# The first slab of the input projection is multiplied with tiles that are not yet normalised

## The chip, the cores and the metric

The kernel runs on one core of a Trainium2 chip. The metric is the device time of one execution in microseconds (us); the shown number is the median of three runs. The engines of the core work side by side, each on its own list of instructions, and wait for each other on semaphores: TensorE (PE, matmuls into the eight PSUM banks), VectorE (DVE), ScalarE (ACT), GpSimd (POOL) and SyncE (SP, which issues the loads of weights).

## The reference

Two transformer-like blocks follow each other on one sequence of 512 tokens and 1024 features in fp32. The part around the change is the end of the first block and the beginning of the second:

```python
# first block, end
x = x + 0.5 * swiglu(rmsnorm(x, ffn2_norm), ffn2_w_gate, ffn2_w_up, ffn2_w_down)
x = rmsnorm(x, final_norm)
# second block, beginning
mod = silu(c) @ ada_w + ada_b                 # shift, scale and gate for each feature
h = rms_norm(x, mix_pre_g) * (1.0 + sc_m) + sh_m
p = h @ w_in                                  # 1024 x 2848: 23 slabs of 128 columns
# rmsnorm(x, g) = x * rsqrt(mean(x*x) + 1e-6) * g, the mean over the features of a token
```

The columns of p feed a gated convolution with 31 taps and, after a mix of each token with the one before it, a recurrence (three lora inputs, then r, k and v).

## The kernel before, in words

**Layout.** Everything lies feature by token: `xT` is eight tiles (KD) of 128 features x 512 tokens. A weight slab is 128 x 1024: the eight 128x128 blocks that make one output tile of 128 columns. Each product is made to nearly fp32 precision from rounded parts: a weight slab is split into `w_hi` and `w_lo`, an activation tile into `h_hi` and `h_lo`, and each block takes three matmuls (hi x hi, hi x lo, lo x hi; `passes`, lines 730 to 732). A slab so costs 24 matmuls of 512 columns.

**Weights.** SP loads slabs into a ring of four; slab n is requested when slab n - 4 has counted up `slab_done`. GpSimd splits each one in order (lines 600 and 602, `w_split`). The slabs of the stretch are `down2` (24: three for each of the eight output tiles), then `in2` (23).

**The seam.** `down(...)` runs the last projection of the first block. Output tile m goes to bank m % 4; VectorE adds it to `xT` (`add_half`, line 2081), ScalarE squares it (`norm_squares`, line 1551), VectorE adds the squares up. When tile 7 is squared, TensorE finishes the sums (`last_sums`, line 850). Two norms follow each other here with nothing between, so their two scales for a token are found together: ScalarE takes the roots (1608, 1609), VectorE the reciprocals (1972, 1974), and TensorE spreads the product of both over the partitions into bank 6 (line 861, `spread`). VectorE scales the tiles with it (`norm_split`, line 2006), ScalarE adds the shift and rounds to `h_hi` (`norm_hi`, line 1627), VectorE makes `h_lo` (line 1996). Tile by tile, `first(2, ...)` multiplies the first two slabs of `in2` (lines 762, 763, 768) into banks 0 and 1; at its end it spreads the scale of the first norm alone into bank 5 ("the second spread").

**Behind it.** `for m in range(2, 23): project(m)` multiplies the other slabs with 24 matmuls each (bank m % 4, lines 730 to 732), and `lora_products(2 * (m - 3), 2 * (m - 3) + 2)` follows `project(m)` for m from 3 to 8 (line 1259). The very first of them waits so:

```python
if n == 0:
    pe.wait_ge(S("lora_in"), 48)
    pe.wait_ge(S("lora_act"), 3)
...
if n == 0:
    pe.wait_ge(S("x_final"), 8)
```

`x_final` counts eight `final_norm` tiles that VectorE makes from `xT` and bank 5 (line 2475). VectorE then clears four margins (2481) and runs `shifted(0)` to `shifted(2)` (line 2266), which finish the three lora inputs that ScalarE has copied out of banks 0, 1 and 2 (`raw_in`, line 1751). ScalarE applies a tanh and two sigmoids to them (lines 1876 to 1878, with two table loads) and counts `lora_act` to 3. All orders are written out by hand; every engine works its list strictly in order.

Of the kernel before, what the change touches and what calls it, by code (L numbers as in the profile page):

```python
# [18 lines left out]
P = 128  # L19
# [61 lines left out]

HI_AT = {"ffn1": 0, "mix": 1, "ffn2": 2, "mixpre": 3, "ffnpre": 4}

# [147 lines left out]
def build(nc, x_in, slabs, ada_in, vec_in, both_in, block1_in, block2_in, rope_in, relb_in, lora_in, g2b_in,  # L231
          y_out):
    ctx = ExitStack()
    with ctx:
# [31 lines left out]
        masks_t = place("masks", 3 * P, F32R, offset=g2b_at)  # L266
        ones_t = masks_t[:, :].bitcast(F32)
        arena = cursor[0]
        acth_t, actl_t = place("act_hi", KF * T, F32R), place("act_lo", KF * T, F32R)
# [4 lines left out]
        masks = {n: masks_t[:, P * i:P * i + P] for i, n in enumerate((64, 32, 128))}  # L274
        act_hi, act_lo = tiles(acth_t, KF), tiles(actl_t, KF)

        def slot(name, at, n, dt=F32, w=T):
# [84 lines left out]
        row_rec = small_t[:, 108:124]  # L362
        keep_mu = small_t[:, 60:75]
        d_end, omka = [small_t[:, 28 + 16 * half:44 + 16 * half] for half in range(2)], small_t[:, 232:236]

# [361 lines left out]
        def _(pe):  # L727
# [20 lines left out]

            def first(count, at, norm, wait_bank, late=None):


                for k in range(KD):
                    if late == "mix" and k == 5:
                        norm_stats(late)
                    for n in range(count):
                        if k == 0:
                            wait_bank(n)
                            pe.wait_ge(S("w_split"), at + n + 1)
                        if n == 0:
                            pe.wait_ge(S("norm_hi"), 8 * HI_AT[norm] + k + 1)  # L760
                        w, r = slice(P * k, P * k + P), (at + n) % RING
                        mm(bank[n], w_hi[:, r, w], h_hi[:, k, :], start=k == 0, stop=False, skip_group_check=True)  # L762
                        mm(bank[n], w_lo[:, r, w], h_hi[:, k, :], start=False, stop=False, skip_group_check=True)  # L763

                    pe.wait_ge(S("norm_lo"), 8 * HI_AT[norm] + k + 1)
                    for n in range(count):
                        w, r = slice(P * k, P * k + P), (at + n) % RING
                        last = mm(bank[n], w_hi[:, r, w], h_lo[:, k, :], start=False, stop=k == KD - 1, skip_group_check=True)  # L768
                        if k == KD - 1:
                            last.then_inc(S("slab_done"), 1)  # L770
# [153 lines left out]
            def down(name, o, done, done_at, norm):  # L924
# [23 lines left out]
                if norm == "ffnpost":  # L948
                    last_row_by_halves()
                    return  # L950
                last_sums(norm)
                pe.wait_ge(S("second_rs"), 1)
                spread(bank[6], both_rs, 1).then_inc(S("second_mm"), 1)


# [502 lines left out]


            first(2, at, "mixpre", lambda n: pe.wait_ge(S("x_new"), 21 + n))  # L1460
            for m in range(2, 23):
                project(m)
# [80 lines left out]
        def _(act):  # L1543
            f = nc.scalar.activation

            def norm_squares(name, src, wait=None):
# [32 lines left out]
                else:  # L1579
                    for j in range(KD - 1 if name == "ffnpost" else KD):  # L1580
# [8 lines left out]
                        if name not in LATE and j == KD - 2:  # L1589

                            f(small_t[:, 254:255], small_t[:, 255:256], ACT.Sqrt)
                        square(j)
                if name == "ffnpost":
                    for half in range(2):
# [12 lines left out]
                if name == "mixpre":  # L1607
                    f(both_std, pre_sums[1], ACT.Sqrt, bias=EPS * EPS, scale=1.0 / D).then_inc(S("second_std"), 1)
                f(n_std, pre_sums[0] if name == "mixpre" else bank[7][:, 0:4], ACT.Sqrt, bias=EPS, scale=1.0 / D)\
                    .then_inc(S("norm_std"), 1)  # L1610

            def late_hi(name, j):
# [127 lines left out]
            for i in range(2):  # L1740
                act.dma_start(lora[:, i, :], lora_in[:, i, :]).then_inc(S("lora_in"), 16)
            norm_hi("mixpre")


            def raw_in(m):
# [3 lines left out]
                if m == 0:  # L1749
                    act.wait_ge(S("keep_mu"), 1)  # L1750
                f(shift_tile(m), bank[n % 4], ACT.Copy, scale=keep_mu[:, mu_of(m):mu_of(m) + 1]).then_inc(S("in2_raw"), 1)
# [192 lines left out]
        def _(dve):  # L1944
# [116 lines left out]
            def gains_made():  # L2061
# [11 lines left out]
                v.tensor_tensor(gp["mixpost"], mod[:, 16:24], vec("mix_post_g", 0, 8), ALU.mult)  # L2073
                v.tensor_tensor(gp["ffnpost"], mod[:, 40:48], vec("ffn_post_g", 0, 8), ALU.mult)

            def add_half(o, at, n_slabs, scale, norm):

                for m in range(KD):
                    sum_squares(norm, m - 1)
                    dve.wait_ge(S("slab_done"), at + n_slabs * (m + 1))  # L2080
                    v.scalar_tensor_tensor(out=xT[:, m, :], in0=bank[m % 4][:, :], scalar=scale, in1=xT[:, m, :],  # L2081
# [172 lines left out]
            gains_made()  # L2254
            add_half(16, SLAB_AT["down2"], 3, 0.5, "mixpre")

            dve.wait_ge(S("block1_in"), 32)
            norm_split("mixpre", gs["mixpre"])
            v.tensor_scalar(keep_mu, vec("mu", 0, 15), -1.0, 1.0, ALU.mult, ALU.add).then_inc(S("keep_mu"), 1)
            link(v.tensor_scalar(omka, vec("k_a", 0, 4), -1.0, 1.0, ALU.mult, ALU.add))  # L2260

# [92 lines left out]
            def recurrence(half):  # L2354
# [97 lines left out]
                if half:  # L2452
                    dve.wait_ge(S("second_std"), 2)
                    for j in range(4):
# [275 lines left out]
```

## Time and profile before

| | |
|---|---|
| median of 3 runs | 1700.24 us (1700.13 to 1701.5) |
| the profiled execution | 1701.04 us, of which the span from first to last instruction is 1699.2 us |
| TensorE busy | 1657.6 us, 98% |
| VectorE, ScalarE, GpSimd busy | 56%, 25%, 58% |
| mean granted clock of TensorE | 0.991 |

Busy times are shares of the span. A matmul's end is modelled and matmuls overlap, so the distance between the starts of two matmuls is the measure of their cost and not the duration shown. The granted clock of a stretch is 1.00 at 2.4 GHz and 0.50 at 1.2 GHz.

### The profile page before, as it was taken

Reading aid. Unit: us, or ns where it says so; the run is one execution under the profiler, and the core shown is the slowest. Engines: PE = TensorE matmul, PEld = TensorE weight load, DVE = VectorE, ACT = ScalarE, POOL = GpSimd, SP = SyncE. Lnnn points to the kernel's source line nnn. Section 1 sums busy time; section 2 is a strip of 40 time slices with the busy share of each in tenths; the row PEclk is TensorE's granted clock in tenths of the full one; section 3 lists DMA queues with packets and bytes.
Section 4 is the critical chain, followed back from the end, with each engine's and each line's share of the span. In section 5 each row is a group of like instructions: output and inputs, shape, how many; then the busy total and the mean of one; then the engine's idle time right before and its main releaser. Section 6 shows DMA issues by size and latency. Waiting matters only on the chain.

```text
span 1699.2 us, 26804 instructions
## 1 busy us (share of the span) xinstructions
PE 1657.6 (98%) x10118; PEld 1355.5 (80%) x10118; DVE 946.7 (56%) x1389; ACT 433.2 (25%) x721; POOL 981.4 (58%) x596
## 2 busy tenths in 40 slices
PE   8999999999999999999999999998989999999998
PEld 6888888888767778888888867887868788888887
DVE  5666551226656346666562159987766766665103
ACT  4000000015866321111100031234353333233001
POOL 3666666766572377666677744611205576666774
PEclk9999999999999999999999989999999899999999
DMA  6444443333241134444443322210002232233332
GB/s 215 142 147 148 146 144 118 102 100 121 87 120 33 50 106 143 142 147 148 148 150 111 100 87 70 92 64 3 3 2 87 75 96 92 97 99 99 101 110 88
DMA packets 52112, 175.43 MB, mean 103 GB/s; under 512 B 6272, under 2 KB 8704, under 8 KB 51904
## 3 DMA queue, kind: packets, MB, share of 16 engines
q1 hardware_dynamic: 43056, 144.64, 26.3%
q10 hardware_dynamic: 8976, 29.63, 5.5%
q8 instruction: 61, 1.00, 0.3%
q14 instruction: 19, 0.16, 0.0%
HBM read 169.46 MB, written 2.10 MB: 101 GB/s over the span
## 4 chain that ended last, share of the span: by engine, by line
PE 93%; ACT 2%; DVE 2%; issue 1%; POOL 1%; DMA 0%; ACTq 0%; SPq 0%; DVEq 0%; POOLq 0%
PE banks L730 25%; PE banks L732 25%; PE banks L731 25%; PE banks L1199 4%; PE banks L1055 1%; PE banks L1028 1%; PE banks L762 1%; PE banks L1039 1%; PE banks L763 1%; PE banks L768 1%; PE banks L850 1%; PE banks L1025 1%; PE banks L1174 1%; PE banks L803 1%; PE banks L805 0%
## 5 line engine op out<-in xcount | busy, mean ns | idle before, releaser
L602 POOL TENSOR_TENSOR w_lo<-w_raw,w_hi 128x1024 fp32r<-128x1024 f32 x256 | 634.2, 2477 | 21.4
L600 POOL TENSOR_SCALAR w_hi<-w_raw 128x1024 fp32r<-128x1024 f32 x256 | 288.4, 1126 | 555.5 <-DMA w_raw<-in_slabs 477.0
L730 PE MATMUL banks<-h_hi,w_hi 128*128 128x512 f32 x1376 | 540.6, 393 | 0.6 <-POOL w_lo L602 0.6
L732 PE MATMUL banks<-h_hi,w_lo 128*128 128x512 f32 x1376 | 535.7, 389 | 0.0
L731 PE MATMUL banks<-h_lo,w_hi 128*128 128x512 f32 x1376 | 535.6, 389 | 0.0
L730 PEld LDWEIGHTS banks<-h_hi,w_hi 128*128 128x128 f32 x1376 | 258.4, 188 | 60.2 <-issue 5.8
L731 PEld LDWEIGHTS banks<-h_lo,w_hi 128*128 128x128 f32 x1376 | 258.4, 188 | 54.4 <-issue 1.7
L732 PEld LDWEIGHTS banks<-h_hi,w_lo 128*128 128x128 f32 x1376 | 258.3, 188 | 54.1
L730 PE MATMUL banks<-act_hi,w_hi 128*128 128x512 f32 (+1 forms) x550 | 209.7, 381 | 0.0
L731 PE MATMUL banks<-act_lo,w_hi 128*128 128x512 f32 (+1 forms) x550 | 209.3, 381 | 0.0
L732 PE MATMUL banks<-act_hi,w_lo 128*128 128x512 f32 (+1 forms) x550 | 209.3, 381 | 0.0
L730 PEld LDWEIGHTS banks<-act_hi,w_hi 128*128 128x128 f32 x550 | 103.4, 188 | 19.7
L731 PEld LDWEIGHTS banks<-act_lo,w_hi 128*128 128x128 f32 x550 | 103.4, 188 | 19.7
L732 PEld LDWEIGHTS banks<-act_hi,w_lo 128*128 128x128 f32 x550 | 103.4, 188 | 19.7
L2041 DVE TENSOR_TENSOR tmp<-banks,tmp 128x512 f32<-128x512 f32 x44 | 30.5, 692 | 148.2 <-PE banks L732 144.6
L1633 ACT ACTIVATE tmp<-tmp 128x512 f32<-128x512 f32 x44 | 27.9, 634 | 329.5 <-DVE tmp L2041 329.4
L2081 DVE SCALAR_TENSOR_TENSOR xT<-banks,xT 128x512 f32<-128x512 f32 x24 | 16.5, 690 | 165.4 <-PE banks L732 165.4
L2033 DVE TENSOR_TENSOR act_lo<-tmp,act_hi 128x512 f32 x66 | 103.9, 1574 | 8.1
L2055 DVE CUSTOM_DVE_ANT_0 adaw<-adaw,silc 128x1024 f32<-128x1024 f32 x48 | 78.9, 1643 | 5.1 <-DMA adaw<-in_ada 4.8
L2599 DVE SCALAR_TENSOR_TENSOR tmp<-banks,vec,tmp 128x511 f32<-128x511 f32 x44 | 32.8, 746 | 75.9 <-ACT tmp L1933 75.8
L1199 PEld LDWEIGHTS banks<-in_arena 64*64 64x64 f32 x1792 | 59.5, 134 | 10.5 <-issue 6.9
L1199 PE MATMUL banks<-in_arena 64*64 64x64 f32 (+1 forms) x1792 | 62.3, 231 | 5.6 <-issue 2.7
(389 smaller groups left out, 1840.8 us busy)
## 6 DMA issues: line engine op xcount, KB each, us to landing
w_raw<-in_slabs SPq DMA_DIRECT2D x260, 512.0 KB, 3.5
adaw<-in_ada ACTq DMA_DIRECT2D x48, 512.0 KB, 3.6
relb<-in_relb ACTq DMA_DIRECT2D x8, 256.0 KB, 2.9
out_y<-xT SPq DMA_DIRECT2D x16, 128.0 KB, 1.8
w_raw<-in_slabs SPq DMA_DIRECT2D x4, 256.0 KB, 5.2
xT<-in_x SPq DMA_DIRECT2D x1, 1024.0 KB, 8.3
block<-in_block ACTq DMA_DIRECT2D x1, 704.0 KB, 6.1
xT<-in_x SPq DMA_DIRECT2D x2, 256.0 KB, 3.8
```

Of the source, the lines that this page charges most:

```text
L600: nc.gpsimd.tensor_scalar(w_hi[:, r, :], w_raw[:, r, :], 1.0, 1.0, ALU.mult, ALU.mult).then_inc(S("w_hi"), 1)
L602: nc.gpsimd.tensor_tensor(w_lo[:, r, :], w_raw[:, r, :], w_hi[:, r, :], ALU.subtract).then_inc(S("w_split"), 1)
L730: mm(out, hi, rhs_hi, start=start, stop=False, skip_group_check=True)
L731: mm(out, hi, rhs_lo, start=False, stop=False, skip_group_check=True)
L732: return mm(out, lo, rhs_hi, start=False, stop=stop, skip_group_check=True)
L762: mm(bank[n], w_hi[:, r, w], h_hi[:, k, :], start=k == 0, stop=False, skip_group_check=True)
L1199: last = mm(out, block_of(lhs, operands, e, g, c), r, start=opens and i == 0, stop=i == len(pairs) - 1, skip_group_check=True)
L1633: f(tmp[:, 2 + u, :], tmp[:, 2 + u, :], ACT.Silu).then_inc(S("silu"), 1)
L2033: v.tensor_tensor(actl_t[:, bass.ds(at * T, T)], t, hi, ALU.subtract).then_inc(S("act_lo"), 1)
L2041: v.tensor_tensor(tmp[:, 2 + u, :], bank[2 * u], tmp[:, 0, :], ALU.mult).then_inc(S("gate_scaled"), 1)
L2055: v.tensor_tensor_reduce(out=adaw[:, u, :], in0=adaw[:, u, :], in1=silc, scale=1.0, scalar=0.0, op0=ALU.mult, op1=ALU.add, accum_out=mod_s ...
L2599: v.scalar_tensor_tensor(out=tmp[:, n, 1:T], in0=bank[n][:, 0:T - 1], scalar=w[1], in1=tmp[:, n, 1:T], op0=ALU.mult, op1=ALU.add).then_inc ...
```

## The change

Slab 0 of `in2` is no longer multiplied with the normalised tiles. ScalarE and VectorE make tiles `act_hi` and `act_lo` from `xT` times the feature's gain alone (`unscaled_hi`, `unscaled_lo`), seven of them before the last down projection's tile is added, the eighth after it. TensorE multiplies slab 0 with them in four places between the steps of the norm (`first_unscaled`), then multiplies the slab with the shift, two columns (`shift_parts`, 16 matmuls), into bank 3. ScalarE copies bank 3's columns and bank 0 out, VectorE multiplies bank 0 with the scale in bank 6 and adds the shift's product. `first` then takes slabs 1 and 2 into banks 1 and 2, and the loop of projections begins at slab 3. `raw_in(0)` and product 3 wait for the repaired bank.

```diff
-HI_AT = {"ffn1": 0, "mix": 1, "ffn2": 2, "mixpre": 3, "ffnpre": 4}
+HI_AT = {"ffn1": 0, "mix": 1, "ffn2": 2, "unscaled": 3, "mixpre": 4, "ffnpre": 5}
...
                 if norm == "ffnpost":
                     last_row_by_halves()
                     return
+                first_unscaled(range(2))
                 last_sums(norm)
+                first_unscaled(range(2, 3))
                 pe.wait_ge(S("second_rs"), 1)
                 spread(bank[6], both_rs, 1).then_inc(S("second_mm"), 1)
+                first_unscaled(range(3, KD))
+                n = SLAB_AT["in2"]
+                for k in range(KD):
+                    w = slice(P * k, P * k + P)
+                    for part in (w_hi, w_lo):
+                        last = mm(bank[3][:, 0:2], part[:, n % RING, w], shift_parts[:, k, :], start=k == 0 and part is w_hi,
+                                  stop=k == KD - 1 and part is w_lo, skip_group_check=True)
+                last.then_inc(S("slab_done"), 1)
+
+            def first_unscaled(ks):
+                n = SLAB_AT["in2"]
+                if 0 in ks:
+                    pe.wait_ge(S("x_new"), 21)
+                    pe.wait_ge(S("w_split"), n + 1)
+                for k in ks:
+                    w = slice(P * k, P * k + P)
+                    pe.wait_ge(S("norm_hi"), 8 * HI_AT["unscaled"] + k + 1)
+                    pe.wait_ge(S("norm_lo"), 8 * HI_AT["unscaled"] + k + 1)
+                    passes(bank[0], w_hi[:, n % RING, w], w_lo[:, n % RING, w], act_hi[:, k, :], act_lo[:, k, :], k == 0, k == KD - 1)
...
-            first(2, at, "mixpre", lambda n: pe.wait_ge(S("x_new"), 21 + n))
-            for m in range(2, 23):
+            first(2, at + 1, "mixpre", lambda n: pe.wait_ge(S("x_new"), 22 + n), begin=1)
+            for m in range(3, 23):
+                if m == 3:
+                    pe.wait_ge(S("keep_mu"), 2)
                 project(m)
...
                         square(j)
+                        if name == "mixpre" and j == KD - 2:
+                            act.wait_ge(S("slab_done"), SLAB_AT["down2"] + 3 * (KD - 1) + 1)
+                            for i in range(KD - 1):
+                                unscaled_hi(i)
+                        if name == "mixpre" and j == KD - 1:
+                            unscaled_hi(j)
...
+            def unscaled_hi(j):
+                f(act_hi[:, j, :], xT[:, j, :], ACT.Copy, scale=gs["mixpre"][:, j:j + 1]).then_inc(S("norm_hi"), 1)
...
             norm_hi("mixpre")
+            act.wait_ge(S("slab_done"), SLAB_AT["in2"] + 1)
+            f(shift_sums, bank[3][:, 0:2], ACT.Copy)
+            f(tmp[:, 0, :], bank[0], ACT.Copy).then_inc(S("second_std"), 1)
...
                 if m == 0:
-                    act.wait_ge(S("keep_mu"), 1)
+                    act.wait_ge(S("keep_mu"), 2)
...
+                link(v.tensor_copy(shift_parts[:, :, 0], shf["mixpre"]))
+                link(v.tensor_tensor(shift_parts[:, :, 1], shf["mixpre"], shift_parts[:, :, 0], ALU.subtract))
+
+            def unscaled_lo(j):
+                dve.wait_ge(S("norm_hi"), 8 * HI_AT["unscaled"] + j + 1)
+                v.scalar_tensor_tensor(out=act_lo[:, j, :], in0=xT[:, j, :], scalar=gs["mixpre"][:, j:j + 1], in1=act_hi[:, j, :],
+                                       op0=ALU.mult, op1=ALU.subtract).then_inc(S("norm_lo"), 1)
...
                     sum_squares(norm, m - 1)
+                    if norm == "mixpre" and m == KD - 1:
+                        for j in range(KD - 1):
+                            unscaled_lo(j)
                     dve.wait_ge(S("slab_done"), at + n_slabs * (m + 1))
...
             add_half(16, SLAB_AT["down2"], 3, 0.5, "mixpre")
+            unscaled_lo(KD - 1)
             dve.wait_ge(S("block1_in"), 32)
             norm_split("mixpre", gs["mixpre"])
             v.tensor_scalar(keep_mu, vec("mu", 0, 15), -1.0, 1.0, ALU.mult, ALU.add).then_inc(S("keep_mu"), 1)
+            dve.wait_ge(S("second_std"), 2)
+            v.tensor_tensor(shift_sum, shift_sums[:, 0:1], shift_sums[:, 1:2], ALU.add)
+            link(v.tensor_tensor(bank[0], tmp[:, 0, :], bank[6], ALU.mult))
+            v.tensor_scalar(bank[0], bank[0], shift_sum, None, ALU.add).then_inc(S("keep_mu"), 1)
```

In `first` the new argument `begin` moves the banks (`bank[begin + n]`); the rest of the diff places the small tiles and moves a later wait on `second_std` from 2 to 3.

## Rows read from the trace of the kernel before

**Rows 1.** The page: engine totals, and the chain that ended last by engine.

```profile
PE 1657.6 (98%) x10118; PEld 1355.5 (80%) x10118; DVE 946.7 (56%) x1389; ACT 433.2 (25%) x721; POOL 981.4 (58%) x596
...
PE 93%; ACT 2%; DVE 2%; issue 1%; POOL 1%; DMA 0%; ACTq 0%; SPq 0%; DVEq 0%; POOLq 0%
```

**Rows 2.** Timeline of TensorE: start, duration, what, count, idle before and its releaser.

```profile
975.60 1.84 PE L850 MATMUL banks<-small,tmp 128*128 128x2 f32 x16
...
977.30 0.49 PE L730 MATMUL banks<-act_hi,w_hi 128*128 128x512 f32 x1
...
979.70 1.87 PE L850 MATMUL banks<-small,tmp 128*128 128x3 f32 x8 [1.45 <-ACT tmp L1551]
...
982.11 1.12 PE L861 MATMUL banks<-both,small 128*128 128x128 f32 x4 [0.54 <-DVE small L1972]
...
984.92 0.77 PE L762 MATMUL banks<-h_hi,w_hi 128*128 128x512 f32 x1 [1.69 <-ACT h_hi L1627]
...
990.88 0.39 PE L762 MATMUL banks<-h_hi,w_hi 128*128 128x512 f32 x1
...
997.69 0.60 PE L861 MATMUL banks<-both,small 128*128 128x128 f32 x4
...
998.04 0.48 PE L730 MATMUL banks<-h_hi,w_hi 128*128 128x512 f32 x1
...
1008.81 0.39 PE L732 MATMUL banks<-h_hi,w_lo 128*128 128x512 f32 x1
...
1009.59 1.13 PE L1259 MATMUL banks<-in_arena 64*128 64x512 f32 x4 [0.39 <-issue]
```

**Rows 3.** Timelines of VectorE, ScalarE and GpSimd through the seam.

```profile
978.29 0.69 DVE L2081 SCALAR_TENSOR_TENSOR xT<-banks,xT 128x512 f32<-128x512 f32 x1 [12.57 <-PE banks L732]
...
979.02 0.63 ACT L1551 ACTIVATE tmp<-xT 128x512 f32<-128x512 f32 x1 [15.44 <-DVE xT L2081]
...
981.88 0.18 DVE L1972 RECIPROCAL small<-small 128x4 f32<-128x4 f32 x1 [2.90 <-ACT small L1608]
...
983.27 1.41 DVE L2006 SCALAR_TENSOR_TENSOR tmp<-xT,mod,banks 128x512 f32<-128x512 f32 x2 [1.15 <-PE banks L861]
...
984.05 1.38 ACT L1627 ACTIVATE h_hi<-tmp,mod 128x512 fp32r<-128x512 f32 x2 [2.21 <-DVE tmp L2006]
...
984.81 0.98 DVE L1996 SCALAR_TENSOR_TENSOR h_lo<-tmp,mod,h_hi 128x512 fp32r<-128x512 f32 x1
...
993.71 1.63 DVE L1996 SCALAR_TENSOR_TENSOR h_lo<-tmp,mod,h_hi 128x512 fp32r<-128x512 f32 x2
...
977.06 2.36 POOL L602 TENSOR_TENSOR w_lo<-w_raw,w_hi 128x1024 fp32r<-128x1024 f32 x1
```

**Rows 4.** Timelines of VectorE and ScalarE behind the second spread.

```profile
998.39 5.36 DVE L2475 SCALAR_TENSOR_TENSOR xT<-xT,vec,banks 128x512 f32<-128x512 f32 x8 [2.62 <-PE banks L861]
...
1005.62 0.74 DVE L2266 SCALAR_TENSOR_TENSOR tmp<-banks,vec,tmp 128x511 f32<-128x511 f32 x1
...
1007.05 1.28 ACT L1877 ACT_TABLE_LOAD   x1
...
1008.88 0.61 ACT L1878 ACTIVATE tmp<-tmp 128x512 f32<-128x512 f32 x1
```

**Rows 5.** Windows of TensorE: stretch, length, busy (count), granted clock, DMA, GB/s.

```profile
978.00:978.50 0.50, 0.26 (x2) 0.98 0.00 0
...
978.50:979.00 0.50, 0.00 (x0) 0.50 0.00 0
...
988.50:989.00 0.50, 0.50 (x3) 0.78 0.00 0
```

**Rows 6.** Windows: busy of PE, PEld, DVE, ACT, POOL, then granted clock.

```profile
1016.00:1126.00 110.00, 110.00 (x459) 84.42 (x459) 101.62 (x144) 25.96 (x41) 53.44 (x31) 1.00 0.27 87
```

**Rows 7.** The chain, a piece of it: start, duration, first matmul at the next norm.

```profile
1324.94 0.77 PE banks L762
```

**Rows 8.** Windows of all engines, at the next norm.

```profile
1330.00:1331.00 1.00, 1.00 (x5) 0.83 (x5) 1.00 (x3) 0.50 (x1) 0.47 (x1) 0.97 0.00 0
```

## What the change will do to the time: the prediction

> **What bounds the kernel now.** I read the engine table and the chain of waits first. TensorE is busy 98% of the span and is 93% of the chain [rows 1], so only TensorE time can be won, and the question is what each stretch of it waits for. Then I went through TensorE's timeline at the seam between the last down projection and the input projection [rows 2], next to VectorE's and ScalarE's [rows 3], to see who ends each wait. The last big product starts at 977.30 and three such matmuls with their start-up end near 978.1. The next big matmul starts only at 984.92. In those 6.8 us stand: the add of tile 7 (978.29), its square (979.02), the sums (979.70, 1.87 us), root and reciprocal (981.88), the spread (982.11), the first scaled tile (983.27) and its rounding (984.05). The granted clock [rows 5] is at its low level, 0.50 (1.2 GHz), from 978.5 and comes back only at about 988.7: the windows row 988.50 to 989.00 has 0.78. From 984.92 to 988.7 TensorE works at half speed, so 3.8 us cost 1.9. The visible price of the seam is 6.8 + 1.9 = 8.7 us. That is what the change aims at.
>
> Then I asked what stands behind the seam, because an earlier product is worth something only if what follows can start. The row that decides is L1259, the first lora product, at 1009.59 with 0.39 us of idle before it [rows 2]. The profile calls that "issue". The code has a wait there for lora_act (three activations) and x_final. On the other engines [rows 4] the third activation starts at 1008.88 and lasts 0.61, so it ends at 1009.49, 0.10 us before the product. Its chain goes back without a hole: the spread into bank 5 starts at 997.69 [rows 2]; VectorE starts the eight final-norm tiles at 998.39 and has them at 1003.75; four memsets and three shifted tiles follow, the last from 1005.62 to 1006.36; then tanh, a table load at 1007.05 (1.28), two sigmoids. So L1259 starts 1009.59 - 997.69 = **11.9 us after the spread starts**, whatever TensorE does in between. Now it has two products in between (2 and 3), 0.35 + 2 x 5.44 = 11.2 us, plus a little, and waits 0.4 to 0.55.
>
> **The change part by part.** One matmul of 512 columns costs 0.227 us at the full clock: from 990.88 to 997.69 lie five steps of six, 1.362 each [rows 2].
>
> *Before the sums.* ScalarE makes seven unscaled hi tiles (0.7 each, 5.0 us) and VectorE seven lo tiles (0.75 to 1.0 each, at most 7 us) after the first slab of row 7 is used. That slab is done 39 matmuls before 975.60, at 966.8, so lo is through at about 974.7. VectorE stood idle 12.57 us before 978.29 and ScalarE 15.44 us before 979.02 [rows 3], so this costs nothing; without that cover the add of tile 7 would be late by what is over. The two small operations that make shift_parts fall before the down projection, where VectorE waits for TensorE. The weight slabs that the seam needs are split by 977.06 + 2.36 = 979.42 at the latest [rows 3] and the first of them well before.
>
> *TensorE through the seam, at full clock.* Two unscaled steps, 6 x 0.227 = 1.36: 978.1 to 979.45. The sums wait for the same square as before: 979.70, now at the fast price of row 975.60 (1.70 for 16, so 0.85 for 8): 980.55. The third step with 0.1 start-up, 0.78: 981.33. ScalarE inserts hi 7 after the square (0.7), and VectorE inserts lo 7 (0.98 as in row 984.81) from 980.4 to 981.4. That stands ahead of its reciprocals, which would be due near 980.8, so it delays them by 0.6 and the spread starts at 981.65 (0.23 behind the reciprocal as now). Spread 0.35: 982.0. Five steps, 3.4 + 0.1: 985.5. The shift's product is 16 matmuls of two columns. The trace has this form only as the sums, 0.106 each, so 1.7; below, it may vanish almost (0); above, it is bounded by a full matmul each, 3.6. I take 1.7, the nearest in columns: 987.2. Then the two-slab loop over scaled tiles, 8 x 1.362 = 10.9, which ends at 998.1. The scaled tiles no longer bound it: the first scaling starts at 982.35 instead of 983.27, the last lo tile is there near 994.4 instead of 995.34 [rows 3] and is wanted at 997.6. So the second spread starts at **998.1, against 997.69: 0.4 us later**, with three slabs done at that point instead of two. This is a gain of 5.44 - 0.4 = 5.0 us of TensorE work.
>
> *Repair of bank 0.* ScalarE adds two copies, VectorE three operations (about 0.16 + 0.7 + 0.75), from 994.8 to 996.5; product 3 waits for it but starts at 998.45. Cover 1.9 us; a longer repair would delay product 3, which has room, as follows. Slab in2+4 is requested earlier, when the shift's product ends, which only helps.
>
> *After the spread.* Only product 3 is left between the spread and L1259: 998.45 to 1003.9. The lora chain starts with the spread at 998.1 and is not shortened by anything in the diff, so L1259 starts at 998.1 + 11.9 = 1010.0, and TensorE stands idle **6.1 us** where it stood 0.4. Queued behind L1259 are product 4 and all others; none can pass. The 5.0 us are thus returned in full, and 0.4 us more. From 1016 to 1126 TensorE is busy 110.00 of 110 us and VectorE 101.62 [rows 6], so lateness there is not taken in later.
>
> *The clock.* The stall is followed by slow matmuls. The trace has two such restarts: 984.92 to 988.7 (3.8 us, costs 1.9), and at the next norm from 1324.94 to about 1330.0, where the windows row 1330 to 1331 has 0.97 [rows 5, 7, 8] (5.1 us, costs 2.5). I take 2.25 for the new stall. The stall's length, 6.1, is near the 6.7 between 978.3 and 984.9 in which the clock stayed low.
>
> The Trainium skill ("TensorE: Matmul & The Clock Gate", HAM oscillation) says that a wait between two bursts throttles the engine again, so that the next burst starts slow; rows 5 agree (0.50 through the wait, and 3.8 us into the next burst). By that rule the change moves the slow restart instead of removing it. The same page (What's actually happening) says the number of slow matmuls varies from run to run; two restarts of 3.8 and 5.1 us in one trace fit that.
>
> **Sum.** 0.4 + 2.25 = 2.65 us. Against the profiled execution, 1701.04 (span 1699.2 and 1.84 around it), this is 1703.7; that execution is 0.8 above the median of the runs, 1700.24, from which it is 1702.9. I take the middle, **1703.3**. What a measurement can tell from no change is 0.2%, 3.4 us, so from 1700.24 the line lies at 1703.64, just above.
>
> **The rivals.**
> *A. The clock falls within the seam as well.* For: in rows 5 it fell by 978.5, only 0.2 us after the last big matmul ended, so the idle time behind cannot have done it alone; the 16 small matmuls from 975.60 stand unchanged, and the change adds 16 more at 985.5. Against: 978.1 to 979.45 is now filled. Slow steps cost 1.9 to 2.5 once more, all before the second spread and therefore all on the path: 1705.2 to 1706.3 (1703.3 + 1.9 to 2.5, and a little for a product of 3.0 instead of 1.7). Chance 0.32.
> *B. As intended.* The place is L1259: if its wait is not the lora chain but something that moves along with TensorE, product 4 follows product 3 at once, 5.0 us are gained and no restart is slow: 1700.24 - 5.0 = 1695.2; with some part of the stall left, up to 1699. Against: 0.10 us between the end of the sigmoid and the product, and a chain without holes [rows 4]. This decides from the point where lora_act is ready before 1003.9. Chance 0.06.
> *C. The stall costs only its 0.4.* The slow restart is short or the shift's product nearly free: 1700.2 to 1702.2. For: low bound 0 of that product. Against: both restarts of the trace. Chance 0.14.
> *D. The new work on VectorE and ScalarE is dearer than its cover* (lo tiles past 978.29, or a table load for the copies between squares and roots): 1 to 3 us on the path, 1704.3 to 1706.5. Against: 12.57 us of idle time, and copies behind the roots that had no load. Chance 0.05.
>
> **How the numbers follow.** The forecast (0.43) has its own range, 1702.3 to 1704.3; a quarter of it lies above 1703.64. Faster by over 0.2% (under 1696.8): most of B, and a rest for what I have missed: 0.06. Slower: A 0.30, D 0.05, the quarter of the forecast 0.11, in all 0.46. Within 0.2%: 0.48. The range, 1701.2 to 1706.5, takes in A, D and the upper half of C, and leaves B out.
>
> **What would show it.** L1259 after more than 5 us of idle time; the last activation 0.1 us before it; the second spread within 1 us of 997.7; the granted clock high through 979 to 998 (low there: A) and low after 1004; no idle time of note before the first unscaled matmul. I am wrong if product 4 follows product 3 closely, if lora_act comes before 1004, or if the 16 two-column matmuls take more than 3 us.

## The result, and the profile after

The kernel after takes 1708.26 us (median of 5 runs, 1707.33 to 1709.45), the kernel before 1700.24 us beside it: the ratio is 1.0045, 95% interval 1.0034 to 1.0056, slower by 8.0 us. Forecast were 1703.3 us and a range of 1701.2 to 1706.5. The direction and the stall came as forecast; the size did not: 1708.26 us lies outside the range.

The page of the kernel after, engine totals [for before: rows 1]:

```profile
PE 1663.5 (98%) x10134; PEld 1355.4 (79%) x10134; DVE 963.8 (57%) x1402; ACT 439.5 (26%) x731; POOL 989.0 (58%) x596
```

TensorE's timeline of the kernel after through the seam and behind it (start, duration, what, count, idle before and its releaser). The lines answer to rows 2; L855 is line 850 of before, L866 is 861, L1286 is 1259, L733 to L735 are 730 to 732, and L966 is the shift's product:

```profile
977.63 1.84 PE L855 MATMUL banks<-small,tmp 128*128 128x2 f32 x16
...
982.64 0.48 PE L733 MATMUL banks<-act_hi,w_hi 128*128 128x512 f32 x1
...
983.43 0.60 PE L866 MATMUL banks<-both,small 128*128 128x128 f32 x4
...
987.32 0.17 PE L966 MATMUL banks<-shift_parts,w_hi 128*128 128x2 f32 x1
...
989.02 0.48 PE L766 MATMUL banks<-h_hi,w_hi 128*128 128x512 f32 x1
...
996.63 0.39 PE L767 MATMUL banks<-h_hi,w_lo 128*128 128x512 f32 x1
997.34 0.74 PE L772 MATMUL banks<-h_lo,w_hi 128*128 128x512 f32 x2 [0.33 <-DVE h_lo L2038]
...
1000.73 0.60 PE L866 MATMUL banks<-both,small 128*128 128x128 f32 x4
1001.49 0.50 PE L733 MATMUL banks<-h_hi,w_hi 128*128 128x512 f32 x1 [0.16 <-DVE banks L2317]
...
1006.84 0.39 PE L735 MATMUL banks<-h_hi,w_lo 128*128 128x512 f32 x1
1012.74 2.08 PE L1286 MATMUL banks<-in_arena 64*128 64x512 f32 x4 [5.51 <-ACT tmp L1920]
1014.75 0.79 PE L733 MATMUL banks<-h_hi,w_hi 128*128 128x512 f32 x1
```

Three things are to be seen. The seam is closed: between 977.63 and 1000.73 TensorE has no hole of more than half a microsecond (the longest is the 0.33 us at 997.34). Three slabs are done at the second spread (1000.73). Then L1286 waits 5.51 us, and the profile now names ScalarE's last activation as the releaser. ScalarE, VectorE and GpSimd in the same execution, in three timelines [rows 3 and 4]. L2038 makes the lo tiles of the norm, L2048 scales a tile with bank 6:

```profile
1003.42 1.28 ACT L1918 ACT_TABLE_LOAD   x1
1009.55 0.63 ACT L1918 ACTIVATE in_arena<-in_arena 64x512 f32<-64x512 f32 x1 [4.85 <-DVE tmp L2324]
1010.20 1.28 ACT L1919 ACT_TABLE_LOAD   x1
...
1012.03 0.62 ACT L1920 ACTIVATE tmp<-tmp 128x512 f32<-128x512 f32 x1
```

```profile
969.66 8.76 DVE L2123 SCALAR_TENSOR_TENSOR act_lo<-xT,mod,act_hi 128x512 fp32r<-128x512 f32 x7 [2.12 <-ACT act_hi L1649]
980.32 0.69 DVE L2134 SCALAR_TENSOR_TENSOR xT<-banks,xT 128x512 f32<-128x512 f32 x1 [1.89 <-PE banks L735]
...
985.61 2.37 DVE L2038 SCALAR_TENSOR_TENSOR h_lo<-tmp,mod,h_hi 128x512 fp32r<-128x512 f32 x1
...
993.02 1.46 DVE L2038 SCALAR_TENSOR_TENSOR h_lo<-tmp,mod,h_hi 128x512 fp32r<-128x512 f32 x1
994.51 0.75 DVE L2048 SCALAR_TENSOR_TENSOR tmp<-xT,mod,banks 128x512 f32<-128x512 f32 x1
995.17 2.11 DVE L2038 SCALAR_TENSOR_TENSOR h_lo<-tmp,mod,h_hi 128x512 fp32r<-128x512 f32 x1
...
1001.54 5.36 DVE L2533 SCALAR_TENSOR_TENSOR xT<-xT,vec,banks 128x512 f32<-128x512 f32 x8
...
1008.77 0.74 DVE L2324 SCALAR_TENSOR_TENSOR tmp<-banks,vec,tmp 128x511 f32<-128x511 f32 x1
```

```profile
985.02 2.42 POOL L605 TENSOR_TENSOR w_lo<-w_raw,w_hi 128x1024 fp32r<-128x1024 f32 x1
...
994.02 2.71 POOL L605 TENSOR_TENSOR w_lo<-w_raw,w_hi 128x1024 fp32r<-128x1024 f32 x1
```

The last activation ends at 1012.65 and L1286 starts at 1012.74, 12.0 us after the second spread: it was 11.9 before. The windows of TensorE (stretch, length, busy, granted clock, DMA, GB/s) show where the clock is low [rows 5]:

```profile
982.00:1000.00 18.00, 17.68 (x90) 1.00 0.22 79
1004.00:1011.00 7.00, 3.23 (x15) 1.00 0.34 119
1011.00:1012.00 1.00, 0.00 (x0) 0.58 0.00 0
1012.00:1013.00 1.00, 0.26 (x2) 0.50 0.00 0
1017.00:1018.00 1.00, 1.00 (x4) 0.51 0.00 0
```

It is at 1.00 through the whole seam, and still until 1011, though the last matmul before the stall started at 1006.84. It falls to 0.50 within the stall and is back only near 1018.0, so L1286 takes 2.0 us instead of 1.06 and the first matmuls of product 4 0.43 instead of 0.23.

**Where the 6.3 us between the two spans lie** (1705.5 - 1699.2). Take the start of an instruction in the trace of after minus the start of the same one before:

| instruction | before | after | difference |
|---|---|---|---|
| a product of the first slabs | 12.29 | 11.51 | -0.78 |
| down projection 1, early | 293.89 | 293.42 | -0.47 |
| a product on cq_lo, in the attention behind it | 410.68 | 411.12 | +0.44 |
| the 16 sums of rows 2 | 975.60 | 977.63 | +2.03 |
| the first lora product | 1009.59 | 1012.74 | +3.15 |
| product 4 | 1010.65 | 1014.75 | +4.10 |
| the same product, clock back | 1012.16 | 1017.48 | +5.32 |
| the last down projection, late | 1646.30 | 1652.75 | +6.45 |

The seam and its stall account for 3.3 us (2.03 to 5.32). About 2.8 us are lost before it, from 12 to 976 us, and 1.1 behind it. There the diff changes no instruction on the path. The difference grows evenly inside the three down projections, by 0.9 to 1.2 us in each, by some 0.5 us in the attention between the first two, and hardly anywhere else. That asked for the experiments.

### The profile page after: what moved, and what is told of

It reads as the page before. It is cut to its first block, busy times and chain, and to the rows that moved or that the text cites. A ratio compares the mean times of both kernels' runs of the same rounds, so it can differ in the third digit from the quotient of the medians.

```text
span 1705.5 us, 26870 instructions
## 1 busy us (share of the span) xinstructions
PE 1663.5 (98%) x10134; PEld 1355.4 (79%) x10134; DVE 963.8 (57%) x1402; ACT 439.5 (26%) x731; POOL 989.0 (58%) x596
## 4 chain that ended last, share of the span: by engine, by line
PE 90%; DVE 4%; ACT 3%; POOL 2%; issue 1%; DMA 1%; ACTq 0%; SPq 0%; DVEq 0%; POOLq 0%
PE banks L733 25%; PE banks L735 25%; PE banks L734 25%; PE banks L1226 4%; PE banks L1055 1%; PE banks L1082 1%; PE banks L855 1%; PE banks L766 1%; PE banks L772 1%; PE banks L1066 1%; PE banks L767 1%; DMA w_raw<-in_slabs 1%; PE banks L1201 1%; DVE h_lo L2038 1%; PE banks L808 0%
## 5 line engine op out<-in xcount | busy, mean ns | idle before, releaser
L603 POOL TENSOR_SCALAR w_hi<-w_raw 128x1024 fp32r<-128x1024 f32 x256 | 293.5, 1147 | 554.0 <-DMA w_raw<-in_slabs 475.9
L733 PE MATMUL banks<-h_hi,w_hi 128*128 128x512 f32 x1368 | 538.2, 393 | 0.7 <-POOL w_lo L605 0.5
L735 PE MATMUL banks<-h_hi,w_lo 128*128 128x512 f32 x1368 | 533.0, 390 | 0.0
L733 PEld LDWEIGHTS banks<-h_hi,w_hi 128*128 128x128 f32 x1368 | 257.2, 188 | 61.5 <-issue 6.5
L735 PEld LDWEIGHTS banks<-h_hi,w_lo 128*128 128x128 f32 x1368 | 257.1, 188 | 54.0
L733 PE MATMUL banks<-act_hi,w_hi 128*128 128x512 f32 (+1 forms) x558 | 215.3, 386 | 0.0
L735 PE MATMUL banks<-act_hi,w_lo 128*128 128x512 f32 (+1 forms) x558 | 213.8, 383 | 0.0
L735 PEld LDWEIGHTS banks<-act_hi,w_lo 128*128 128x128 f32 x558 | 104.7, 188 | 22.6
L733 PEld LDWEIGHTS banks<-act_hi,w_hi 128*128 128x128 f32 x558 | 104.9, 188 | 19.2
L2134 DVE SCALAR_TENSOR_TENSOR xT<-banks,xT 128x512 f32<-128x512 f32 x24 | 16.6, 691 | 161.0 <-PE banks L735 161.0
L2075 DVE TENSOR_TENSOR act_lo<-tmp,act_hi 128x512 f32 x66 | 100.0, 1514 | 8.1
L2088 DVE TENSOR_TENSOR tmp<-tmp 128x512 f32<-128x512 f32 x44 | 65.3, 1484 | 8.6 <-ACT tmp L1672 8.6
```

The source lines that it names most:

```text
L603: nc.gpsimd.tensor_scalar(w_hi[:, r, :], w_raw[:, r, :], 1.0, 1.0, ALU.mult, ALU.mult).then_inc(S("w_hi"), 1)
L733: mm(out, hi, rhs_hi, start=start, stop=False, skip_group_check=True)
L735: return mm(out, lo, rhs_hi, start=False, stop=stop, skip_group_check=True)
L2075: v.tensor_tensor(actl_t[:, bass.ds(at * T, T)], t, hi, ALU.subtract).then_inc(S("act_lo"), 1)
L2088: v.tensor_tensor(tmp[:, 4 + u, :], tmp[:, 2 + u, :], tmp[:, 4 + u, :], ALU.mult)\
```

## The experiments

Every run is compared with runs of the kernel before on the same chip; its ratio to them has a 95% interval. Times are medians. The intervals reach 0.1% or so to each side, some 1.5 us, so a difference of a few tenths of a microsecond is read from the traces and not from the times.

**The place of shift_parts.** The change puts a tile of 64 bytes per partition ahead of `act_hi` and `act_lo`. `after_end` puts it behind them:

```diff
-        shift_t = place("shift_parts", 2 * KD, F32R)
         arena = cursor[0]
         acth_t, actl_t = place("act_hi", KF * T, F32R), place("act_lo", KF * T, F32R)
+        shift_t = place("shift_parts", 2 * KD, F32R)
```

> The kernel after, with one thing moved: the 64 bytes per partition of shift_parts lie behind act_lo instead of ahead of act_hi, so that the large tiles act_hi, act_lo and all that shares their place start at the same address as before the change. Theory P (placement): products whose moving tile lies there take 0.229 us a matmul in the profile after, against 0.2255 before, in all three down projections, also in the one long before the changed code; by the offsets between the two traces that is 1.2 us from 285 to 565, 1.2 us from 565 to 966 and about 1 us at the end, 3.3 us in all. It expects 0.229 to go back to 0.2255 and 1708.3 - 3.3 = 1705.0 us. Rival: the offset ahead of the seam is a difference between two executions, or comes from something else in the changed code; then the time stays at 1708.3 and the pitch at 0.229. Both expect the stall of 5.5 us before the first lora product to stay, with slow matmuls behind it.

Measured: 1704.93 us against 1700.84, ratio 1.0024 (1.0015 to 1.0034), 3.3 us less than after. The stall of 5.51 us stays. `before_pad64` is the other side of it:

```diff
+        cursor[0] += 64
         arena = cursor[0]
```

> The kernel before, with 64 unused bytes per partition ahead of act_hi and nothing else changed. Theory P: the act matmuls go from 0.2255 to 0.229 us, the time from 1700.2 to 1703.5 us. Rival: no change, 1700.2 us.

Measured: 1705.09 us, ratio 1.0024 (1.0014 to 1.0033), 4.2 us slower without any other change. So the 64 bytes alone cost 3.3 us (from after to after_end, by the medians; 3.9 if each is taken against before beside it) to 4.2 us (here). I had taken the distance to a multiple of 128 bytes for the rule:

> The kernel before, with 128 unused bytes per partition ahead of act_hi. Theory P, in the form that what matters is where the address lies within 128 bytes: no change to before, 1700.8 us, with 0.2255 us a matmul. Rival: any other address, or a longer distance between the tiles of the kernel, costs as 64 bytes did: 1704.5 us and 0.229.

Measured (`cursor[0] += 128`): 1711.01 us, ratio 1.0061 (1.0047 to 1.0075), beside 1700.34. My form of the theory is refuted: 128 bytes cost not nothing but 10.7 us. Two runs looked for the period and for what the address is relative to:

> The kernel before with 256 unused bytes per partition ahead of act_hi. 64 bytes cost 4.2 us and 128 bytes 10.7 us, against the form of theory P that I held. Theory P256: what counts is where act_hi and act_lo lie within 256 bytes; then 256 bytes cost nothing, 1700.3 us. Rival: the cost grows with the distance or has a longer period; then 1704 us or more.

Measured (`cursor[0] += 256`): 1700.63 us against 1701.10, ratio 1.0000 (0.9991 to 1.0009). No cost.

```diff
-        base = -(-nc.sbuf_base // 64) * 64
+        base = -(-nc.sbuf_base // 64) * 64 + 128
```

> The kernel before with every tile of the core's memory moved up by 128 bytes, act_hi, act_lo, h_hi, h_lo and the weights alike. Theory R: what costs is the place of the moving tile relative to the weights that TensorE loads beside it; that is unchanged here, so 1700.3 us. Theory A: what costs is the tile's own address; then the act matmuls (1650 of them, 0.233 instead of 0.2265 us) cost their 10 us again, and with them the 4128 matmuls on h_hi and h_lo, which now lie as act_hi did in before_pad128, 27 us more: 1737 us.

Measured: 1700.19 us against 1701.10, ratio 0.9998 (0.9989 to 1.0006). No cost, so the tile's own address is not what counts. The last run splits the tiles at another place:

```diff
+        cursor[0] += 128
         w_at = cursor[0]
```

> The kernel before with 128 unused bytes per partition between h_lo and the weights: the weights, the small tiles and act_hi, act_lo move up together, xT, h_hi and h_lo stay. Theory W (what costs is where the moving tile lies relative to the weights, within 256 bytes): the products on h_hi and h_lo now have the distance that those on act_hi and act_lo had in before_pad128 and take 0.233 us instead of 0.2265, 4128 of them 27 us more, while those on act_hi and act_lo keep their pace: about 1728 us. Rival H: act_hi and act_lo were slow there because of their distance to xT, h_hi or h_lo; then the act products are slow again and the others not, 1711 us. Rival: neither, 1701 us.

Measured: 1725.69 us against 1700.69, ratio 1.0145 (1.0128 to 1.0162), 25.0 us slower. The windows of TensorE show which products pay. The columns are as above; the number behind x counts the matmuls in 80 us with those that reach over an edge of the window. A few per cent of records can be missing, so a step of one or two says nothing. The first and third windows lie in down projections (moving tiles act_hi, act_lo), the second in a gate-and-up stage (h_hi, h_lo). The kernel before:

```profile
270.00:350.00 80.00, 80.00 (x355) 1.00 0.33 104
640.00:720.00 80.00, 80.00 (x355) 1.00 0.46 151
885.00:965.00 80.00, 80.00 (x355) 1.00 0.33 108
```

The kernel after:

```profile
270.00:350.00 80.00, 80.00 (x352) 1.00 0.32 103
640.00:720.00 80.00, 80.00 (x355) 1.00 0.45 151
885.00:965.00 80.00, 80.00 (x351) 1.00 0.33 106
```

`before_pad128`:

```profile
270.00:350.00 80.00, 80.00 (x345) 1.00 0.31 99
640.00:720.00 80.00, 80.00 (x354) 1.00 0.44 148
885.00:965.00 80.00, 80.00 (x345) 1.00 0.32 103
```

`before_w128`:

```profile
270.00:350.00 80.00, 80.00 (x355) 1.00 0.33 107
640.00:720.00 80.00, 80.00 (x348) 1.00 0.43 147
885.00:965.00 80.00, 80.00 (x355) 1.00 0.34 111
```

355 matmuls in 80 us become 352 and 351 in after and 345 in before_pad128, in the down projections alone. In before_w128 it is the other way round: the act products are back at 355 and the h products fall to 348. The distances between the starts of two matmuls say it more sharply. These are their means in ns, over 265 to 365 and 885 to 965 us for the act products and 640 to 720 us for the h products, worked out from the traces with distances over 0.3 us (missing records) left out:

| kernel | distance of the act tiles to the weights, modulo 256 bytes | act products | h products |
|---|---|---|---|
| before, after_end, before_pad256, before_base128 | 0 | 226.7 | 226.7 |
| after, before_pad64 | 64 | 228.9 | 226.7 |
| before_pad128 | 128 | 233.3 | 226.7 |
| before_w128 | 0 (of the h tiles: 128) | 226.7 | 232.4 |

The distance follows from the sizes of the tiles in the kernel: in before the weights begin 49,152 bytes behind xT and act_hi begins 118,016 bytes behind it, 68,864 bytes apart, which is 269 times 256. w_hi lies 16,384 bytes behind w_raw and w_lo, and act_lo 45,056 behind act_hi, multiples of 256 too. What the slow products have in common is a distance between moving tile and weights that is not a multiple of 256 bytes. The granted clock is 1.00 in all of these windows and TensorE is never idle there, which is why neither a wait nor the clock shows this cost.

One rival is left: GpSimd and the loads work on the same weight tiles, and the distance to their traffic could be what counts. The same traces answer it. In before_pad128 the act products are 233.3 ns apart where GpSimd splits beside them (596 distances) and 233.4 where it does not (176); in before_w128 the h products are 232.4 and 232.3 apart (251 and 90). Where no load is under way, the act products of before_pad128 are 233.4 apart (379). So the cost needs neither.

**The stall behind the seam.** `after_end_later` issues each pair of lora products one projection later:

```diff
-                if 3 <= m <= 8:
-                    lora_products(2 * (m - 3), 2 * (m - 3) + 2)
+                if 4 <= m <= 9:
+                    lora_products(2 * (m - 4), 2 * (m - 4) + 2)
```

> The kernel of after_end, with each pair of lora products one projection later. Theory S: product 4 (5.4 us) fills the stall of 5.5 us, the clock stays high, so 5.5 + 2.2 = 7.7 us less than after_end, 1697.3 us, 3 us below the kernel before. Rival: what the change costs is made of waits within the seam (the repair of bank 0, lo tiles late), and the stall only shows them; then a stall of a few us stays before the first lora product or comes up elsewhere, and the time is above 1702 us.

Measured: 1698.13 us against 1700.84, ratio 0.9984 (0.9975 to 0.9993), 6.8 us less than after_end. The same edit to the kernel before is the control:

> The kernel before, with each pair of lora products issued one projection later (after products 4 to 9 instead of 3 to 8). Theory S (the first lora product waits for a chain of 11.9 us that starts with the second spread): the wait of 0.4 to 0.55 us goes and nothing else changes, since TensorE had only that much to wait: 1699.7 us. Rival: the later lora products delay the gates and the convolution behind them on VectorE, which has 8 us of room in 110, and the time rises by 1 us or more.

Measured: 1700.15 us, ratio 0.9999 (0.9990 to 1.0008). So the order of the lora products is worth next to nothing without the change and 6.8 us with it. The waits of TensorE in after_end_later, from 975 to 1130 us (us in total, times, longest), show what is late next:

```profile
PE banks L733 <- DVE in_arena L2324: 1.0, 1, 1.0
PE banks L1201 <- DVE in_arena L2324: 0.3, 1, 0.3
PE banks L772 <- DVE h_lo L2038: 0.2, 1, 0.2
```

The 1.0 us is product 4, which writes bank 0 and waits until `shifted(0)` has read it (L2324). VectorE comes to that only behind the eight final-norm tiles. `after_end_shifted` tests the chain from this side, without moving the lora products:

```diff
+            for m in range(3):
+                shifted(m)
             for j in range(KD):
                 final_norm(j)
             for j in range(4):
                 link(v.memset(conv_in[:, j, 0:32], 0.0))
-            for m in range(3):
-                shifted(m)
```

> The kernel of after_end with one order changed on VectorE: the three shifted lora inputs come ahead of the eight final-norm tiles instead of behind them. Theory S: the chain to the third activation gets 5.9 us shorter, and the first lora product then waits for the last final-norm tile (its other wait), about 3 us earlier than now: 1701.9 us, and 1699.7 if the shorter stall (2.4 us) also keeps the clock up. Rival: the stall is made by something else than this chain, and the time stays at 1704.9.

Measured: 1701.27 us against 1700.34, ratio 1.0001 (0.9992 to 1.0010). By the medians that is 0.9 us above before (by the ratio 0.2), where after_end was 4.1 above: 3.2 us less. Its waits, same columns:

```profile
PE banks L1286 <- DVE xT L2533: 2.6, 1, 2.6
PE banks L772 <- DVE h_lo L2038: 0.3, 1, 0.3
```

The stall went from 5.5 to 2.6 us, and its releaser is now the last final-norm tile, the other wait of the code, as expected. The clock still fell, in a stall of 2.6 us: of its windows, 1008 to 1009 has 0.50, and 1011 to 1012 has 1.00 again.

A window of after_end_shifted, columns as for TensorE above:

```profile
1008.00:1009.00 1.00, 1.00 (x5) 0.50 0.00 0
```

**The clock as a term of its own.** `after_end_fill` puts 24 useless matmuls into the stall (their result is not used):

```diff
                 project(m)
+                if m == 3:
+                    pe.wait_ge(S("w_split"), at + 5)
+                    for i in range(24):
+                        mm(bank[7], w_hi[:, (at + 4) % RING, P * (i % KD):P * (i % KD) + P], h_hi[:, i % KD, :], ...)
```

> The kernel of after_end with 24 more matmuls of 512 columns between product 3 and the first lora product, into the unused bank 7: work that is thrown away, 5.45 us of it, in the 5.5 us in which TensorE would stand still. The stall itself stays for the rest. Theory C (the clock is a term of its own): the granted clock stays high through the stall, the first lora product starts when it did, and the slow restart goes, 2.2 us less than after_end's 1704.9: 1702.7 us. Rival: the slow restart costs nothing beyond the stall, since VectorE's work behind it is the limit; then the useless matmuls change nothing, 1704.9 us, or add a few tenths.

Measured: 1701.76 us against 1700.34, ratio 1.0006 (0.9997 to 1.0015): 1.4 us above before, where after_end was 4.1 above. That is 2.7 us less for more work. One window of each (columns as above), first after_end, then after_end_fill:

```profile
1011.00:1012.00 1.00, 1.00 (x4) 0.50 0.00 0
```

```profile
1011.00:1012.00 1.00, 1.00 (x6) 1.00 0.00 0
```

Both first lora products start at 1010.04 in the profiles. Only the clock differs, 0.50 against 1.00 at 1011, so the slow restart is a cost of its own: 2.7 us by the runs, 2.2 in the profile of after. The difference of 2.7 is one of two comparisons on two chips, each with an interval of 0.1% to either side; the two traces, 0.1 us apart ahead of the seam, are 2.6 us apart near 1040 us, 2.7 us in all.

**GpSimd in the norm.** In the timelines of after, VectorE's lo tiles beside GpSimd's splits take 2.37, 1.46 and 2.11 us instead of 0.75. The scaling at 994.51, which lies beside the same split but reads one of its two tiles from a PSUM bank, keeps its 0.75. The second of these splits belongs to slab in2+4. The change requests it earlier: its split starts at 992.88, or 990.9 with the 2.0 us of offset taken off, against 1001.24 before. `after_end_later_hold` holds that load back:

```diff
                 sp.wait_ge(S("slab_done"), n + 1 - RING)
+                if n == SLAB_AT["in2"] + 4:
+                    sp.wait_ge(S("norm_lo"), 8 * HI_AT["mixpre"] + KD)
```

> The kernel of after_end_later, with the load of slab in2+4 held back until all normalised lo tiles are made. In the profiles after the change GpSimd splits this slab within the norm, and VectorE's lo tiles beside it take 1.5 and 2.1 us instead of 0.75. Theory G (GpSimd's split slows VectorE through the memory they share): the lo tiles beside it go back to 0.75, VectorE is through the norm about 2 us earlier, TensorE loses its wait of 0.2 to 0.4 us in the loop and the second spread comes 0.5 to 0.8 us earlier: 1697.4 us. Rival: the long lo tiles are none of GpSimd's doing, and stay; or the held slab becomes late itself and the time rises above 1698.1.

Measured: 1697.25 us against 1700.34, ratio 0.9978 (0.9969 to 0.9987). Against before beside it that is 3.1 us less, where after_end_later had 2.7 less. The intervals overlap; the time does not settle it. The traces do. In after_end_later the two lo tiles beside the split of slab in2+4 take 1.45 and 2.11 us; with that split held back they are:

```profile
990.23 0.75 DVE L2040 SCALAR_TENSOR_TENSOR h_lo<-tmp,mod,h_hi 128x512 fp32r<-128x512 f32 x1
...
991.68 0.74 DVE L2040 SCALAR_TENSOR_TENSOR h_lo<-tmp,mod,h_hi 128x512 fp32r<-128x512 f32 x1
```

The first lo tile, beside the split before it, which was not held, stays long (2.38 us). The wait of 0.2 us for a lo tile is gone, and the second spread starts 16.6 us behind the first instead of 17.2. It does not all reach the end, because the wait of product 4 is longer:

```profile
PE banks L735 <- DVE in_arena L2326: 1.3, 1, 1.3
```

**All together.** `best` is after_end_later_hold with the order of after_end_shifted:

> The kernel of after_end_later_hold with the three shifted lora inputs ahead of the final-norm tiles on VectorE. In the profile of after_end_later_hold product 4 waits 1.3 us for bank 0, which shifted(0) frees only behind the eight final-norm tiles. Theory S: that wait goes, and the time from 1697.3 to 1696.0 us. Rival: the final-norm tiles, now 2 us later, hold up the first lora product instead, and nothing is won.

Measured: 1696.07 us against 1701.10 (7 and 23 runs), ratio 0.9972 (0.9961 to 0.9983): 5.0 us below the kernel before and 12 below after. Its window from 965 to 1020 us:

```profile
965.00:1020.00 55.00, 54.94 (x262) 1.00 0.29 96
```

TensorE is busy 54.94 of 55 us there at clock 1.00 (50.93 at 0.91 in before), and the wait of product 4 is gone. The lo tiles that took 1.46 and 2.11 us in after are at 0.75, as in after_end_later_hold. The Trainium skill ("GPSIMD Engine Reference", 1. Specifications) says that GpSimd shares its memory interfaces with VectorE and that they contend when a VectorE instruction has two inputs in that memory. Lo tiles have two such inputs and were slowed beside a split (1.45 to 2.5 us against 0.75); the scaling with one such input was not (0.75). The traces agree.

## Why the prediction was wrong, step by step

**The step that failed: the small tiles were priced at nothing.** The prediction took account of the two operations that fill shift_parts and of no other effect of the tile. It asked of each edit what instructions and waits it adds, and an edit that only moves addresses has none. The 64 bytes moved act_hi and act_lo off the distance to the weights at which the products keep their pace of 226.7 ns: 3.3 to 4.2 us, half of the 8.0 and more than the whole forecast of 2.65. No rival had it either; D, "dearer than its cover", speaks of engines and not of places. With it added, 1703.3 becomes 1706.6 to 1707.5, near the lowest run (1707.33).

**The stall: right in kind and in place.** L1286 waits 5.51 us (forecast 6.1) for the last activation, which ends 0.09 us before it. Rival B (as intended) is refuted by after_end_later and after_end_shifted together: the wait follows the chain when the chain is shortened and disappears when the consumer is moved. Not seen was that product 4 has a second wait on the same work of VectorE, through bank 0. "Product 4 follows product 3 at once" would not have held even without the lora products.

**Through the seam: TensorE's steps within 0.3 us but one, VectorE's not.** With the 2.03 us of offset taken off, the first spread starts at 981.40 (forecast 981.65), the shift's product at 985.3 (985.5) and lasts 1.70 us (1.7), and the two-slab loop starts at 987.0 (987.2). The loop takes 11.71 us (989.02 to 1000.73) where 8 x 1.362 = 10.9 was forecast. Two terms were mis-sized in it. The lo tiles were to be through at 994.4 and were so at 997.6: three of them ran beside splits and took 3.7 us more together. The sentence "Slab in2+4 is requested earlier, which only helps" is the one mistake, and after_end_later_hold shows what it is worth; the split of slab in2+3 is the other: it was there before too, but the first lo tile now falls into the midst of it. TensorE so waits for a lo tile (0.71 us between the starts at 996.63 and 997.34 where 0.23 is usual, 0.5 of the 0.8 us), and the second spread comes 1.0 us later than before and not 0.4. The chain behind it takes 12.0 us instead of 11.9, and L1286 is 1.1 us later than before. The repair of bank 0 is late as well (VectorE is free at 1001.51, and product 3 starts 0.76 us behind the spread instead of 0.35), but this costs nothing: the stall comes after it.

The seven unscaled lo tiles took 8.76 us where at most 7 were allowed. The cover held them: VectorE then waited 1.89 us for the last slab, so rival D did not come about.

**The clock: the term right, rival A wrong.** The restart costs 2.2 us in the profile (2.25 forecast) and 2.7 in the comparison of runs. The clock did not fall in the seam (1.00 from 982 to 1000): the 16 small matmuls ahead of the sums and the 16 behind were no danger once the rest was filled. Rival A argued from the fall 0.2 us behind the last big matmul in before; in after the clock was still at 1.00 3.8 us behind it. What decides when it falls is not shown.

**Sum.** Forecast 0.4 + 2.25 = 2.65. In the trace of after the same two terms are 1.1 + 2.2 = 3.3; by the runs they are 4.1 (after_end against before, 2.6 to 5.8 by its interval), and 3.3 to 4.2 for the place come on top. The seam itself gave its gain: three slabs are done at the second spread, which comes 1.0 us later, 5.44 - 1.0 = 4.4 us of TensorE work, all given back in the stall. In best, where the spread comes 0.3 us later (22.4 us behind the 16 sums, against 22.1 in before) and nothing is given back, the runs show 5.0.

## What to carry to other kernels

Work moved ahead of a seam is only a gain if the next thing behind it can start: take the fixed chain that ends in the next wait, and count how much work is left to cover it. A stall that appears costs a second time in the clock of the work behind it. And a new small tile ahead of large ones is not free: here, place it behind them, or keep the distance between a product's moving tile and its weights a multiple of 256 bytes.

## What the runs showed of the hardware

The pace of a 512-column fp32r product depends on the distance in bytes between its moving tile and its weights, with TensorE busy throughout and the clock at 1.00. In the traces two matmuls start 226.7 ns apart where the distance is a multiple of 256 bytes, 228.9 where it is 64 bytes off and 232.4 to 233.3 where it is 128 off. By the kernels' times 64 bytes cost 4.2 us, with 1650 matmuls on the act tiles, 128 bytes 10.7 us with the same and 25.0 us with 4128, and 256 bytes nothing. Moving all tiles together by 128 bytes cost nothing. The runs don't show why, nor whether 192 bytes cost as 64 do, nor whether other types or widths behave so. The small tiles moved with the weights in before_w128, but no product on the h tiles reads them.

VectorE's making of a lo tile, which reads two tiles in the core's memory outside PSUM, takes 1.4 to 2.5 us beside GpSimd's split of a slab and 0.75 alone. Holding one split back brought the second spread 0.55 us forward in the traces; what that is worth in the kernel's time (0.4 us between two comparisons) lies within the intervals and stays open.
